# Turning the FFNs' activations on VectorE and through DRAM instead of on TensorE

## What is computed

```python
def swiglu(h, w_in, w_out):
    gu = h @ w_in                       # 256x2048 @ 2048x11008
    g, u = jnp.split(gu, 2, axis=-1)
    return (jax.nn.silu(g) * u) @ w_out # 256x5504 @ 5504x2048
...
h = rmsnorm(x, ffn1_norm_pre[l])
x = x + 0.5 * rmsnorm(swiglu(h, ffn1_w_in[l], ffn1_w_out[l]), ffn1_norm_post[l])
```

## Time and profile before

| | us |
|---|---|
| median of 3 runs | 2047.99 |
| lowest and highest | 2047.64, 2048.58 |
| the profiled execution | 2048.64 |
| its span, first to last instruction | 2047.0 |
| TensorE busy | 2022.8 |
| VectorE busy | 1332.8 |
| ScalarE busy | 1046.1 |
| GpSimd busy | 24.7 |

### The profile page before, as it was taken

The page is one execution under the profiler, slowest core; times in us unless marked ns, Lnnn a source line. Parts: engine busy times, 40 slices in busy tenths (PEclk is TensorE's granted clock), DMA queues, the critical chain, the costliest instruction groups (busy, mean ns, idle before and its releaser), DMA issues.

```text
span 2047.0 us, 23728 instructions
## 1 busy us (share of the span) xinstructions
PE 2022.8 (99%) x9326; PEld 1677.9 (82%) x9326; DVE 1332.8 (65%) x1470; ACT 1046.1 (51%) x1342; POOL 24.7 (1%) x34
## 2 busy tenths in 40 slices
PE   8999999999999999999999999999999999999998
PEld 6888888888888878888888888878888888988886
DVE  6788878756554474456655665588878886555554
ACT  6555555545444454445555554465555554444443
POOL 0000000000000000000100000000000000000000
PEclk9999999999999999999999999999999999999999
DMA  6666666656555645555554456556666666565553
GB/s 234 211 221 200 203 198 216 226 166 221 186 187 187 221 154 190 175 187 163 165 161 148 165 190 210 175 169 211 201 209 197 209 229 200 159 238 189 193 187 123
DMA packets 199174, 392.70 MB, mean 192 GB/s; under 512 B 7409, under 2 KB 15778, under 8 KB 198562
## 3 DMA queue, kind: packets, MB, share of 16 engines
q1 hardware_dynamic: 198610, 388.16, 57.6%
q10 hardware_dynamic: 464, 3.15, 0.4%
HBM read 389.19 MB, written 2.10 MB: 191 GB/s over the span
## 4 chain that ended last, share of the span: by engine, by line
PE 96%; DVE 2%; DMA 1%; ACT 1%; issue 0%; POOL 0%; DVEq 0%; ACTq 0%
PE acc L510 17%; PE acc L512 17%; PE acc L511 17%; PE acc L594 11%; PE acc L596 11%; PE acc L595 11%; PE tp L595 3%; PE tp L596 3%; PE tp L594 3%; PE tp L537 2%; PE tp L765 1%; DMA gain<-in_ffn_norm_post 1%; PE tp L739 1%; DVE w_lo L1156 1%; PE tp L749 0%
## 5 line engine op out<-in xcount | busy, mean ns | idle before, releaser
L1156 DVE TENSOR_TENSOR w_lo<-raw,w_hi 128x1024 fp32r<-128x1024 f32 x408 | 497.0, 1224 | 456.4 <-ACT w_hi L852 439.1
L852 ACT ACTIVATE w_hi<-raw 128x1024 fp32r<-128x1024 f32 x408 | 428.8, 1058 | 442.3 <-PE acc L512 438.2
L874 ACT ACTIVATE w_hi<-raw 128x1024 fp32r<-128x1024 f32 (+1 forms) x400 | 404.9, 1024 | 345.6 <-PE acc L596 241.5
L1189 DVE TENSOR_TENSOR w_lo<-raw,w_hi 128x1024 fp32r<-128x1024 f32 (+1 forms) x400 | 467.3, 1180 | 165.2 <-ACT w_hi L874 162.9
L594 PE MATMUL acc<-w_hi,h_hi 128*128 128x512 f32 (+1 forms) x928 | 356.4, 384 | 0.7 <-DVE w_lo L1189 0.5
L596 PE MATMUL acc<-w_hi,h_lo 128*128 128x512 f32 (+1 forms) x928 | 354.3, 382 | 0.0
L595 PE MATMUL acc<-w_lo,h_hi 128*128 128x512 f32 (+1 forms) x928 | 354.1, 382 | 0.0
L510 PE MATMUL acc<-w_hi,h_hi 128*128 128x512 f32 x736 | 293.9, 399 | 8.4 <-DVE w_lo L1156 6.5
L512 PE MATMUL acc<-w_hi,h_lo 128*128 128x512 f32 x736 | 288.2, 392 | 0.0
L511 PE MATMUL acc<-w_lo,h_hi 128*128 128x512 f32 x736 | 287.4, 390 | 0.0
L510 PE MATMUL acc<-w_hi,a_hi 128*128 128x512 f32 x688 | 268.2, 390 | 2.1 <-DVE w_lo L1156 2.1
(11 more groups left out here) (146 smaller groups left out, 1740.5 us busy)
## 6 DMA issues: line engine op xcount, KB each, us to landing
raw<-in_ffn_w_in SPq DMA_DIRECT2D x126, 1024.0 KB, 5.1
raw<-in_w_in SPq DMA_DIRECT2D x68, 1024.0 KB, 5.2
raw<-in_ffn_w_out SPq DMA_DIRECT2D x56, 1024.0 KB, 5.1
raw<-in_ffn_w_in SPq DMA_DIRECT2D x68, 512.0 KB, 4.0
raw<-in_ffn_w_out SPq DMA_DIRECT2D x40, 768.0 KB, 4.3
raw<-in_w_out SPq DMA_DIRECT2D x16, 1024.0 KB, 5.0
raw<-in_ffn_w_in SPq DMA_DIRECT2D x16, 768.0 KB, 4.3
raw<-in_ffn_w_in SPq DMA_DIRECT2D x32, 256.0 KB, 4.2
```

The source lines that it names most:

```text
L852: nc.scalar.activation(w_hi[:, s % 4], raw[:, g % 4, s % 2 * 2:s % 2 * 2 + 2], ACT.Copy)\
L874: nc.scalar.activation(w_hi[:, s % 4, 0:n], raw[:, g % 4, s % 2 * 2:s % 2 * 2 + n], ACT.Copy)\
L1156: nc.vector.tensor_tensor(w_lo[:, s % 4], raw[:, g % 4, s % 2 * 2:s % 2 * 2 + 2], w_hi[:, s % 4].bitcast(F32), ALU.subtract).then_inc(lo_r ...
L1189: nc.vector.tensor_tensor(w_lo[:, s % 4, 0:n], raw[:, g % 4, s % 2 * 2:s % 2 * 2 + n], w_hi[:, s % 4, 0:n].bitcast(F32), ALU.subtract).the ...
```

## The change

TensorE no longer turns the FFNs' activations. For each pair VectorE transposes the 32x32 blocks of `stage` into `blocks` (`turn_blocks`), right after `stage` is made and before the next w_lo. GpSimd then issues a DMA of `blocks` (512 KB, 128 partitions of 4 KB) to a DRAM tensor `bounce`, waits for its landing, and issues 16 DMAs that read it back into `a_raw`, each of 32 partitions with 8 pieces of 128 bytes (`move_blocks`), and waits for all 16 before it takes the next pair. The pieces put the 32x32 blocks in their places, so that `a_raw` holds the full transpose, in the order of tokens. `a_raw` is the room of `a_lo`.

ScalarE rounds `a_raw` to `a_hi` before its third step of the next pair's up half (`round_a`, which waits for `blocks_in`), and VectorE makes `a_lo` in place before its own third step (`rest_of_a`). For the last pair this is before steps 7 and 8 of `down`. `down` waits for `a_ready` where it waited for `piece_out`. ScalarE's silu waits for `blocks_turned` where it waited for `turned`. `blocks` takes the room of `dist` and `junk`, so GpSimd makes `dist` after the first FFN's activations are split (`distances`), and it moves blocks between root instructions. In the mixing block, and in the turns of x, z and the heads, nothing is changed.

```diff
-PC_BC = PC_A + 2 * (PAIRS + 1)
+PC_BC = PC_A
...
+        a_raw = sb("a_raw", [P, FT, SEQ], F32, r_act + 4 * FT * SEQ)
...
+        blocks = sb("blocks", [P, MT * CW], F32, r_dist)
+        bounce = nc.dram_tensor("bounce", (P, MT * CW), F32, kind="Internal").ap()
+        short_bounce = nc.dram_tensor("short_bounce", (P, MT * TAIL), F32, kind="Internal").ap()
...
+        def pair_tiles(a, i, m):
+
+            tiles = min(4, FT - 4 * i)
+            return a[:, 4 * i:4 * i + tiles, m * P:(m + 1) * P]
...
+            def distances():
+
+                gp.wait_ge(a_ready, 2 * (PAIRS + 1))
+                for kind in range(2):
...
+            def move_blocks(k):
+
+                for i in range(PAIRS + 1):
+                    n = (PAIRS + 1) * k + i + 1
+                    width, held = (CW, bounce) if i < PAIRS else (TAIL, short_bounce)
+                    gp.wait_ge(blocks_turned, 2 * n)
+                    gp.dma_start(held, blocks[:, 0:2 * width]).then_inc(blocks_out, 16)
+                    gp.wait_ge(blocks_out, 16 * n)
+                    rows_of = held.rearrange("(q c) (b x r) -> b q c x r", q=4, b=4, r=32)
+                    tiles = width // P
+                    for b in range(4):
+                        dst = a_raw[32 * b:32 * b + 32, 4 * i:4 * i + tiles, :].rearrange(
+                            "c t (m q r) -> c q (t m) r", m=MT, q=4)
+                        for q in range(4):
+                            gp.dma_start(dst[:, q], rows_of[b, q]).then_inc(blocks_in, 16)
+                    gp.wait_ge(blocks_in, 256 * n)
...
+                if n == R_PRE[0]:
+                    move_blocks(0)
+                    distances()
+                elif n == R_PRE[2]:
+                    move_blocks(1)
...
-                def turn_last(i):
-                    if i - 1 in FAST_PAIRS:
-                        pe.wait_ge(stage_ready, 2 * fast_count(k, i))
-                    else:
-                        pe.wait_ge(acc_free[1], 2 * (uses[1] + i))
-                    turn_stage(pc + 2 * (i - 1))
...
-                        side(i, GATE_AT[i], gate, gate_bank, None, {2: lambda: turn_last(i)})
+                        side(i, GATE_AT[i], gate, gate_bank, None, {})
...
-                        late = {len(subs) - (3 if len(subs) > 8 else 2): lambda: pe.wait_ge(piece_out, pieces)}
+                        late = {len(subs) - (3 if len(subs) > 8 else 2): ready}
...
+            down(B8, [U_B, U_B], from_a, HIDDEN_SUBS, lambda: pe.wait_ge(a_ready, 2 * (PAIRS + 1)), None, turn_first)
...
+            def round_a(k, i):
+                act.wait_ge(blocks_in, 256 * ((PAIRS + 1) * k + i + 1))
+                for m in range(MT):
+                    nc.scalar.activation(pair_tiles(a_hi, i, m), pair_tiles(a_raw, i, m), ACT.Copy).then_inc(a_hi_ready, 1)
...
-                        ffn_steps(b8, f, GATE_AT[i], UP_AT[i] - GATE_AT[i], last_hi(i))
-                    act.wait_ge(turned, pc + 2 * i)
+                        ffn_steps(b8, f, GATE_AT[i], UP_AT[i] - GATE_AT[i], {})
+                    if i:
+                        act.wait_ge(blocks_turned, 2 * ((PAIRS + 1) * f + i))
+                    else:
+                        act.wait_ge(turned, pc)
...
-                    before = {}
+                    before = {2: lambda: round_a(f, i - 1)} if i else {}
...
-            down(B8, 3, 0, ffn1_norm_post, SC_BC, tail_hi(PC_A))
+            down(B8, 3, 0, ffn1_norm_post, SC_BC, {7: lambda: round_a(0, PAIRS)})
...
+            def turn_blocks(k, i, m, width):
+
+                if (PAIRS + 1) * k + i:
+                    dve.wait_ge(blocks_out, 16 * ((PAIRS + 1) * k + i))
+                tiles = width // P
+                nc.vector.transpose(blocks[:, 0:2 * width].rearrange("p (b t m c) -> p m b t c", b=4, m=MT, t=tiles)[:, m],
+                                    stage[:, m, 0:width].rearrange("p (t b c) -> p b t c", b=4, t=tiles))\
+                    .then_inc(blocks_turned, 1)
+
+            def rest_of_a(k, i):
+                for m in range(MT):
+                    dve.wait_ge(a_hi_ready, 2 * ((PAIRS + 1) * k + i) + m + 1)
+                    nc.vector.tensor_tensor(pair_tiles(a_lo, i, m), pair_tiles(a_raw, i, m), pair_tiles(a_hi, i, m).bitcast(F32),
+                                            ALU.subtract).then_inc(a_ready, 1)
...
-                                  {**(fixes(i) if i in FAST_PAIRS else {}), 4: last_lo(i)})
+                                  fixes(i) if i in FAST_PAIRS else {})
...
+                        before[2] = lambda: rest_of_a(f, i - 1)
...
+                        for m in range(MT):
+                            dve.wait_ge(stage_ready, 2 * fast_count(f, i) + m + 1)
+                            turn_blocks(f, i, m, width)
...
-            down(B8, 3, 0, 0.5, tail_lo(PC_A, 0))
+            down(B8, 3, 0, 0.5, {8: lambda: rest_of_a(0, PAIRS)})
```

More of the change, by code:

```diff
@@ L325, in layer_kernel @@
         sums_ready = sem("sums_ready")
+        blocks_turned = sem("blocks_turned")
+        blocks_out = sem("blocks_out")
+        blocks_in = sem("blocks_in")
+        a_hi_ready = sem("a_hi_ready")
+        a_ready = sem("a_ready")
         combined = sem("combined")
@@ L465, in _ @@
             nc.gpsimd.memset(half[:], -0.5).then_inc(consts_made, 1)
[L466 to L479 removed]
+            def distances():
+                gp.wait_ge(a_ready, 2 * (PAIRS + 1))
+                for kind in range(2):
+                    nc.gpsimd.iota(dist[:, kind, 0:P], pattern=[[-1, P]], base=0, channel_multiplier=1,
+                                   allow_small_or_imprecise_dtypes=True)
+                    link(nc.gpsimd.iota(dist[:, kind, P:3 * P], pattern=[[-1, 2 * P]], base=P, channel_multiplier=1,
+                                        allow_small_or_imprecise_dtypes=True))
+                    for lo, n, b in ((0, P, 0), (P, 2 * P, P)):
+                        d = dist[:, kind, lo:lo + n]
+                        link(nc.gpsimd.affine_select(out=d, in_=d, compare_op=ALU.is_ge, fill=MASKED, base=b,
+                                                     pattern=[[-1, n]], channel_multiplier=1))
+                        if kind:
+                            link(nc.gpsimd.affine_select(out=d, in_=d, compare_op=ALU.is_ge, fill=MASKED,
+                                                         base=WINDOW - 1 - b, pattern=[[1, n]],
+                                                         channel_multiplier=-1))
@@ L653, in gate_up, with down @@
                          {2 * begun: lambda: begin_shared(i)} if begun else {})
-            def turn_tail(pc, uses):
-                def hook():
-                    pe.wait_ge(acc_free[1], 2 * (uses[1] + PAIRS + 1))
-                    turn_stage(pc + 2 * PAIRS, TAIL // P)
-                return hook
-            def down(b8, uses, lhs, subs, pieces, turn_last=None, turn_first=None):
+            def down(b8, uses, lhs, subs, ready, turn_last=None, turn_first=None):
                 def two(t, hook):
@@ L700, in _ @@
             turn_first, hooks = boundary(PC_BC, updated(0), x_tile)
-            down(B8, [U_B, U_B], from_a, HIDDEN_SUBS, PC_BC, turn_tail(PC_A, [0, 0]), turn_first)
+            down(B8, [U_B, U_B], from_a, HIDDEN_SUBS, lambda: pe.wait_ge(a_ready, 2 * (PAIRS + 1)), None, turn_first)
             def turn_qk(c, par, i):
@@ L832, in _ @@
             turn_first, hooks = boundary(PC_EF, updated(1), x_tile)
-            down(E8, U_E, from_z, FULL_SUBS, PC_EF, turn_z(NG), turn_first)
+            down(E8, U_E, from_z, FULL_SUBS, lambda: pe.wait_ge(piece_out, PC_EF), turn_z(NG), turn_first)
             gate_up(F8, PC_F, U_F, hooks)
-            down(H8, U_H, from_a, HIDDEN_SUBS, PC_F + 2 * (PAIRS + 1), turn_tail(PC_F, U_F))
+            down(H8, U_H, from_a, HIDDEN_SUBS, lambda: pe.wait_ge(a_ready, 4 * (PAIRS + 1)))
         @block.scalar
@@ L1135, in _ @@
             gate_up(F8, PC_F, U_F, 2, boundary(SC_EF, 2))
-            down(H8, 3, 2, ffn2_norm_post, None, tail_hi(PC_F))
+            down(H8, 3, 2, ffn2_norm_post, None, {7: lambda: round_a(1, PAIRS)})
         @block.vector
@@ L1352, in gate_up @@
                                                        op0=ALU.mult, op1=ALU.mult).then_inc(acc_free[1], 1)
-            def tail_lo(pc, skip):
-                n = TAIL // P
-                return {5: lambda: plain_lo(pc + 2 * PAIRS, skip,
-                                            lambda m: a_hi[:, 4 * PAIRS:4 * PAIRS + n, m * P:(m + 1) * P],
-                                            lambda m: a_lo[:, 4 * PAIRS:4 * PAIRS + n, m * P:(m + 1) * P], n)}
+                    for m in range(MT):
+                        dve.wait_ge(acc_free[1], 2 * (uses[1] + i) + m + 1)
+                        turn_blocks(f, i, m, width)
             def down(b8, units, k, factor, first=None):
@@ L1594, in _ @@
             gate_up(F8, PC_F, NO_SPLIT, U_F, 2, boundary(2))
-            down(H8, 3, 2, 0.5, tail_lo(PC_F, NO_SPLIT))
```

(1 more changed line is left out.)

28 lines of the change are left out of this document (3 added, 25 removed).

## The result

The changed kernel takes **2043.22 us** (median of 16 runs, 2041.18 to 2045.65) against 2048.11 for the kernel before (16 runs, 2047.64 to 2048.60). The ratio is 0.9977, with a 95% interval of 0.997 to 0.9984. So it is 0.23% faster, where 116 us more were forecast. The profiled execution took 2045.4 us with a span of 2043.5, so it is one of the slower ones, 2.2 us above the median. The runs of the changed kernel scatter over 4.5 us, those of the kernel before over 1 us.

The account below looks back on a forecast made before the run. TensorE, busy 99% of the span, was taken as the bound. Round-trip stalls of 135 us for both FFNs less 18.9 us of transposes gave 116 us more on 2047.99, so 2164 us; range 2034 to 2370.

Parts of the forecast that it names:

- the issue on GpSimd: GpSimd's 17 DMA issues per round trip: 1.2 us each, between SyncE's 0.37 to 0.55 and a root instruction's 1.60.
- the stalls of the full pairs: ScalarE's wait for returned data, per FFN: 47.6 us in pairs 1 to 7, 5.0 in pair 8, 5.4 in pair 10.
- C: Round trip from blocks_turned to blocks_in through DRAM: 17 x 1.2 + 3.0 + 2.5 = 25.9 us.
- Rival 1: Round trip hidden: GpSimd issues like SyncE, 11 us, under every limit; 13.3 us saved, 2034.7 us; chance 0.17.
- The landings: DMA landings in the round trip: 3.0 us for the write to DRAM, 2.5 us for the last read.
- The tipping point: Where both FFNs' stalls equal the 18.9 us saved: a round trip of 20.1 us, an issue of 0.86 us.
- The limit: Longest round trip before TensorE waits in the up half: 19.1 us in pairs 1 to 7.
- The short pair: Last pair, data wanted in the down phase: limit 16.1 us, round trip 25.6, so 9.5 us late per FFN.
- The 6 I take six eighths of it, 0.66: The short pair's 6 stage transposes on TensorE: 0.66 us saved, six eighths of a full pair's 0.88.
- TensorE's part: Stage transposes leaving TensorE: 20 x 0.88 + 2 x 0.66 = 18.9 us off.
- The insertion: a_hi and a_lo moved to the up half's third step: w_lo 0.4 us late in pairs 1 to 7, 5.6 us in all.
- Rival 2: DMA engines bound the round trip: 4096 small pieces take 24.3 us or twice that; about 2263 to 2780 us; chance 0.13.

Follow-up runs that it names:

- the run with the long delay: Changed kernel with four spare GpSimd root instructions between the write's landing and the first read of every pair; 2131.55 us, ratio 1.0407.
- eight DMAs: Changed kernel with each pair's round trip in four writes of 128-byte pieces and four reads of 4 KB rows instead of seventeen DMAs; 2038.57 us.
- The version without late waits: Changed kernel, gain's wait at first use, short pair's a_hi/a_lo at down steps 14 and 15, full pairs' in the gate half of the pair after next; 2026.60 us.

## Why the prediction was wrong

**The step that failed is the issue on GpSimd.** The prediction took 1.2 us for each of 17 issues and asked for one under 0.86 to be wrong in sign. It is 0.58 us, just above SyncE's 0.37 to 0.55, the lower bound. That term is 9.8 us instead of 20.4. The analogy was the error: the 1.59 us of a root instruction on GpSimd say nothing of what it needs to issue a DMA. So the stalls of the full pairs, 7 x 6.8 + 5.0 + 5.4 us an FFN in the sum, are not there, and TensorE is busy for 98% of the span, not 94%. With 0.58 in its place, the prediction's own sum gives C = 17 x 0.58 + 3.0 + 2.5 = 15.4, no stall in any pair, and Rival 1's 2034.7 us. A chance of 0.17 for that case was too little, since the only rows of a DMA issue all stood on its side. Its estimate from the Trainium skill's page "DMA: Bandwidth & Descriptors" (SWDGE vs HWDGE vs iDMA; Latency and other measured facts), 1 us an issue, erred the same way: it took the 1 us to the first byte as time of the issuing engine, which the trace puts at 0.58. (Its 22.5 us give 2096 by the prediction's sum, not 2093.)

**The landings** were taken too short: 3.0 and 2.5 us. In pair 2 there are 0.6 us until GpSimd issues the write, 4.0 until it issues the first read, 9.2 for the sixteen issues and 4.8 from the end of the last to its landing, 18.6 us against the 15.4. So Rival 1's "11 us, under every limit" was wrong too: with 19.4 to 19.5 allowed, the round trip fits by 0.2 to 1.6 us in pairs 2 to 7, at most 0.1 us for each of 17 issues. The tipping point of 0.86 us an issue rested on the short landings. A delay of 5.7 us, which is 0.34 for each issue, already cost 88 us.

**The limit was right** in the pairs with the copy to t, 19.1 against 19.5 us shown. So was the mechanism of a wait that holds up w_hi behind it, as the run with the long delay shows.

**The short pair was late** as the prediction said, by a limit of 16.1, though for another reason. Its data come 20.7 and 20.4 us after they are turned (480.03 to 500.7, 1795.52 to 1815.97). The write lands 5.6 and 5.7 us after its start and the last read some 5 us after its issue has ended, while the gain's 1 MB and the weights load: the DMA share is 1.03 to 1.07 from 1805 to 1815. The 9.5 us over the limit, counted with C = 25.6, became 4.6 and 4.3, of which TensorE shows 1.59 and 3.11 as idle, being late itself from the gain's wait. With eight DMAs the wait vanishes. Rival 1's 2034.7 us with these 8.9 added would be 2043.6, close to the measured time by luck: of the 8.9 TensorE shows 4.7 as idle, and the rest is the gain's wait and the clock.

**Nothing was counted for the gain.** "The 6 I take six eighths of it, 0.66" was credited for each short pair. But TensorE already idled 1.08 and 1.06 us there behind the gain. It now comes there sooner, and the gain lands 7.8 and 7.6 us after its issue instead of 7.3 and 7.2, so the idle times are 2.30 and 2.09 us. That TensorE idled there stood in the trace of the kernel before.

**TensorE's part was right**: 18.9 us forecast, (42.21 against 43.12) 0.91 in a full pair. The version without late waits wins 21.8 us (2048.40 to 2026.60), of which 2.5 are the gain's; the other 19.3 are 20 x 0.91 and 2 x 0.62, which is 19.4. **VectorE's transposes** take 1.30 us a pair (1.29 forecast) and no idle time of TensorE in the gate and up stages stands behind them. **The insertion** in the up half costs 0.29 us a pair instead of 0.4. The stage transposes of TensorE are 88, as said.

**Rival 2 falls.** By the packet counts, 4.4% of 16 engines' 2043.5 us is 1439 us of engine time, 65 for each of 22 round trips and 4 us spread over 16 engines, where the rival had 24.3 for the reads alone. The weights' loads of 1024 KB land in 5.0 to 5.1 us at the median, as before, not in 10. The queue's 14304 packets are far fewer than the 88064 pieces of the reads alone (20 x 4096 + 2 x 3072): many pieces share a packet. The warning of the Trainium skill's page "VectorE: DVE Perf Modes" (The three transpose paths), 19 times slower, is for a large innermost stride at the destination. It is not borne out for whole pieces of 128 bytes.

**The net**: the ten full pairs save 9.1 us an FFN and pay 7 x 0.29 = 2.0 for the insertion; the down stages, which without late waits are 2.0 us shorter than before, are 4.2 and 6.5 us longer in the traced execution. In FFN 2, 2.09 + 3.11 us idle and 2.6 of lower clock are 7.8 of the 8.5 us over 229.74; 0.7 is not itemised. In FFN 1, 2.30 + 1.59 us idle and 1.4 of lower clock after the first are 5.3 of 6.1.

## What to carry to other kernels

Where one number decides the sign, look first for rows of the same kind of instruction: here those of another engine (0.37 to 0.55 us) were near to the 0.58, and those of the same engine (1.59) were not. A result under a limit can be just under it: measure how much is left before building on it. Ask at each place where the bound engine is relieved which wait stands there already, however small: time won ahead of it is idled away. Remove late waits together, and measure them together: one alone may only collect the idle time at the next, and pay for the clock as well.
